# Expert weights through a ring of ten raw pieces, with the expert loops written out

## What is computed

```python
def ec_moe(h, router_w, w_gate, w_up, w_down):
    B, T, D = h.shape
    cap = EC_CAPACITY * T // N_EXPERTS
    aff = jax.nn.softmax(jnp.einsum('btd,de->bte', h, router_w, preferred_element_type=jnp.float32), axis=-1)
    gate, idx = lax.top_k(jnp.swapaxes(aff, 1, 2), cap)
    flat = idx.reshape(B, N_EXPERTS * cap)
    xg = jnp.take_along_axis(h, flat[..., None], axis=1).reshape(B, N_EXPERTS, cap, D)
    a = jax.nn.silu(jnp.einsum('becd,edf->becf', xg, w_gate)) * jnp.einsum('becd,edf->becf', xg, w_up)
    y = jnp.einsum('becf,efd->becd', a, w_down) * gate[..., None].astype(h.dtype)
    return jnp.zeros_like(h).at[jnp.arange(B)[:, None], flat].add(y.reshape(B, N_EXPERTS * cap, D))
```

## Time and profile before

| | |
|---|---|
| median of the runs | 1538.47 us |
| profiled execution, its own time | 1540.21 us |
| its span (first to last instruction) | 1538.4 us |
| PE busy | 1361.9 us, 89% |
| PE weight loads | 1012.9 us, 66% |
| DVE busy | 1017.8 us, 66% |
| ACT busy | 704.7 us, 46% |
| GpSimd busy | 295.8 us, 19% |
| DMA | 296.06 MB, mean 192 GB/s |
| expert stage | from the first gather at 932 to the end |

### The profile page before, as it was taken

The page is one execution under the profiler, slowest core; times in us unless marked ns, Lnnn a source line. Parts: engine busy times, 40 slices in busy tenths (PEclk is TensorE's granted clock), DMA queues, the critical chain, the costliest instruction groups (busy, mean ns, idle before and its releaser), DMA issues.

```text
span 1538.4 us, 18265 instructions
## 1 busy us (share of the span) xinstructions
PE 1361.9 (89%) x6828; PEld 1012.9 (66%) x6828; DVE 1017.8 (66%) x1093; ACT 704.7 (46%) x674; POOL 295.8 (19%) x193
## 2 busy tenths in 40 slices
PE   6888988799698989877889996999999999999995
PEld 1577868688696979662767763666666666666663
DVE  1766124543675959691425366999988999988993
ACT  2322234444334434431322103766667666776672
POOL 1021001111000000000000100135344444554422
PEclk9899989899799999958889967999999999999998
DMA  9403201112302121315106236999999999999992
GB/s 364 141 28 114 81 24 50 50 36 76 97 1 90 55 89 55 103 55 213 38 28 234 97 133 242 353 364 376 372 371 372 366 380 355 373 369 365 367 363 59
DMA packets 111843, 296.06 MB, mean 192 GB/s; under 512 B 7077, under 2 KB 33061, under 8 KB 111785
## 3 DMA queue, kind: packets, MB, share of 16 engines
q1 hardware_dynamic: 108264, 284.25, 50.7%
q0 software_dynamic: 3520, 11.01, 3.1%
HBM read 278.47 MB, written 16.78 MB: 192 GB/s over the span
## 4 chain that ended last, share of the span: by engine, by line
PE 69%; DVE 16%; issue 6%; ACT 6%; DMA 2%; POOL 1%; DVEq 0%; ACTq 0%; SPq 0%; POOLq 0%
PE ps L1547 18%; PE ps L1548 17%; PE ps L1549 17%; PE ps L1613 5%; PE ps L1717 4%; DVE w_lo L1474 3%; ACT w_hi L1016 2%; PE ps L1668 1%; DVE w_lo L1068 1%; ACT arena L841 1%; ACT w_hi L837 1%; DVE arena L1490 1%; DMA arena<-in_w_mod_dram 1%; PE ps L1792 1%; DVE arena L1117 1%
## 5 line engine op out<-in xcount | busy, mean ns | idle before, releaser
L1474 DVE TENSOR_TENSOR w_lo<-arena,w_hi 128x2048 fp32r<-128x2048 f32 x192 | 435.3, 2287 | 67.5 <-ACT w_hi L1016 49.9
L1547 PE MATMUL ps<-w_hi,act_hi 128*80 128x512 f32 (+1 forms) x1048 | 419.7, 401 | 32.1 <-DVE w_lo L1474 14.9
L1548 PE MATMUL ps<-w_lo,act_hi 128*80 128x512 f32 (+1 forms) x1048 | 414.9, 396 | 0.0
L1549 PE MATMUL ps<-w_hi,act_lo 128*80 128x512 f32 (+1 forms) x1048 | 413.6, 395 | 0.0
L1016 ACT ACTIVATE w_hi<-arena 128x2048 fp32r<-128x2048 f32 x180 | 343.4, 1915 | 141.7 <-PE ps L1549 141.7
L1547 PEld LDWEIGHTS ps<-w_hi,act_hi 128*80 128x80 f32 (+1 forms) x1048 | 169.0, 161 | 118.5 <-DVE w_lo L1474 29.7
L1549 PEld LDWEIGHTS ps<-w_hi,act_lo 128*80 128x80 f32 (+1 forms) x1048 | 168.7, 161 | 75.7 <-issue 1.6
L1548 PEld LDWEIGHTS ps<-w_lo,act_hi 128*80 128x80 f32 (+1 forms) x1048 | 169.0, 161 | 69.0 <-issue 1.2
L1547 PE MATMUL ps<-act_hi,w_hi 128*128 128x320 f32 x576 | 189.6, 329 | 5.3 <-DVE act_lo L1375 5.3
L1548 PE MATMUL ps<-act_lo,w_hi 128*128 128x320 f32 x576 | 183.5, 319 | 0.0
L1549 PE MATMUL ps<-act_hi,w_lo 128*128 128x320 f32 x576 | 183.2, 318 | 0.0
(11 more groups left out here) (195 smaller groups left out, 1385.8 us busy)
## 6 DMA issues: line engine op xcount, KB each, us to landing
arena<-in_w_exp_gate_dram SPq DMA_DIRECT2D x64, 1024.0 KB, 8.9
arena<-in_w_exp_up_dram SPq DMA_DIRECT2D x64, 1024.0 KB, 7.2
arena<-in_w_exp_down_dram SPq DMA_DIRECT2D x64, 1024.0 KB, 7.1
arena<-in_w_mod_dram SPq DMA_DIRECT2D x24, 1024.0 KB, 6.4
arena<-in_w_in_dram SPq DMA_DIRECT2D x18, 1024.0 KB, 5.5
arena<-in_w_in_dram SPq DMA_DIRECT2D x12, 512.0 KB, 4.7
gl_raw<-arena SPq DMA_DIRECT2D x32, 160.0 KB, 1.8
arena<-gl_raw SPq DMA_DIRECT2D x8, 640.0 KB, 8.0
```

Of the source, the lines that this page charges most:

```text
L1474: v.tensor_tensor(Wl[sl], eraw[slot], Wh[sl].bitcast(F32), ALU.subtract).then_inc(s_el, 1)
L1547: t.matmul(out, sh, mh, start=start, stop=False)
L1548: t.matmul(out, sh, ml, start=False, stop=False)
L1549: return t.matmul(out, sl, mh, start=False, stop=stop)
```

## The change

The raw ring gets ten pieces: one more over `v_hg` and G1 (slot 0), one over the end of the constants and the states (slot 7), and two in `X` behind the expert's temporaries (slots 8 and 9). Piece 0 is issued right behind the stores of x1, ahead of the stores of the normed rows. Pieces 1 to 3 go out where 0 to 2 did, 4 to 6 where 3 to 5 did; 7 waits for the second half of G2 to be made, 8 for the router's products, 9 for the top-k. From piece 10 on, SP waits for the low part of the piece ten before. All loops over experts are written out in Python, on all five engines. The converted ring keeps its three pairs (`EWh`, `EWl`, `NEW` are other names for the same).

```diff
@@ -203,8 +203,9 @@
         assert 4864 <= 5120
 
         G2s = G2
-        NRE = 6
-        eraw = [part(0, 2048), part(2048, 2048), part(4096, 2048)] + raw
+        eraw = [arena[:, o_vso:o_vso + 2048]] + [part(b, 2048) for b in (0, 2048, 4096)] + raw
+        eraw += [arena[:, o_st - 1024:o_st + 1024], part(7808, 2048), part(9856, 2048)]
+        NRE = len(eraw)
         ye = part(6144, 1024)
         xgt = part(7168, 640)
         xgt3 = xgt.rearrange("p (k t) -> p k t", k=KD)
@@ -217,6 +218,8 @@
         brow = arena[:, o_vso + 2048:o_vso + 2560]
         yq = [v_hg, arena[:, o_vso + 2560:o_vso + 5120].rearrange("p (i n) -> p i n", i=NT)]
         kctx = yq[1][:, 0, :]
+
+        EWh, EWl, NEW = Wh, Wl, NHL
 
         xh, xl = (w[:, 0, :].rearrange("p (k t) -> p k t", k=KD) for w in (act_hi, act_lo))
         xh1, xl1 = (w[:, 2, :].rearrange("p (k t) -> p k t", k=KD) for w in (act_hi, act_lo))
@@ -606,6 +609,14 @@
         def width(key):
             return 1024 if key[0] == "q" else 2048
 
+        def piece_of(n):
+            if n < 8:
+                return n // 4, 0, n % 4
+            e, j = (n - 8) // 12 + 1, (n - 8) % 12
+            if e == NE:
+                return 2, NE - 1, j
+            return j // 4, e - (j >= 8), j % 4
+
         block = ctx.enter_context(nc.Block())
 
         @block.sync
@@ -696,42 +707,38 @@
             for i in range(NT):
                 sp.wait_ge(s_x1, NT + i + 1)
                 sp.dma_start(y_tile[i], x1[:, i, :]).then_inc(s_yrow, 16)
+            wg, wu, wd = (A[n][0] for n in ("w_exp_gate", "w_exp_up", "w_exp_down"))
+
+            def epiece(n):
+                w, e, k = piece_of(n)
+                src = (wg, wu, wd)[w][e, 2 * P * k:2 * P * k + 2 * P, :].rearrange("(k p) n -> p k n", p=P)
+                sp.dma_start(eraw[n % NRE].rearrange("p (k n) -> p k n", k=2), src).then_inc(s_er[n % NRE], 16)
+
+            epiece(0)
             for i in range(NT):
                 sp.wait_ge(s_xn2, i + 1)
                 sp.dma_start(xn_rows[i * P:(i + 1) * P, :], xn2[i % 2]).then_inc(s_xrow[i % 2], 16)
             load(len(PIECES) - 1)
 
 
-            wg, wu, wd = (A[n][0] for n in ("w_exp_gate", "w_exp_up", "w_exp_down"))
-
-            def epiece(w, e, k, slot):
-                src = w[bass.ds(e, 1), bass.ts(k, 2 * P), :].rearrange("a (k p) n -> p (a k) n", p=P)
-                sp.dma_start(eraw[slot].rearrange("p (k n) -> p k n", k=2), src).then_inc(s_er[slot], 16)
-
-
             sp.wait_ge(s_yrow, 16 * NT)
             sp.wait_ge(s_xn2, NT)
             sp.wait_ge(s_sq2, NT)
-            for n in range(8):
-                if n == NRE - NRAW:
-                    sp.wait_ge(s_lo, len(SPLITS))
-                    sp.wait_ge(*used[("mod", LATE[-1], 1)])
-                if n >= NRE:
-                    sp.wait_ge(s_el, n - NRE + 1)
-                epiece(wg if n < 4 else wu, 0, n % 4, n % NRE)
-            with sp.Fori(1, NE) as e:
-                for j in range(12):
-
-                    sp.wait_ge(s_el, e * 12 + (j - 4 - NRE + 1))
-                    if j < 4:
-                        epiece(wg, e, j, (j + 2) % NRE)
-                    elif j < 8:
-                        epiece(wu, e, j - 4, (j + 2) % NRE)
-                    else:
-                        epiece(wd, e - 1, j - 8, (j + 2) % NRE)
-            for j in range(4):
-                sp.wait_ge(s_el, 188 + j - NRE + 1)
-                epiece(wd, NE - 1, j, (188 + j) % NRE)
+            for n in range(1, 4):
+                epiece(n)
+            sp.wait_ge(s_lo, len(SPLITS))
+            sp.wait_ge(*used[("mod", LATE[-1], 1)])
+            for n in range(4, 7):
+                epiece(n)
+            filled(sp, ("g2", LATE[-1]))
+            epiece(7)
+            filled(sp, ("rt",))
+            epiece(8)
+            sp.wait_ge(s_gi, 1)
+            epiece(9)
+            for n in range(NRE, 12 * NE):
+                sp.wait_ge(s_el, n - NRE + 1)
+                epiece(n)
             sp.wait_ge(s_scat, 32 * NE)
             sp.wait_ge(s_nk, 16)
             sp.wait_ge(s_nv, 16)
@@ -809,7 +816,7 @@
             gather(1)
             gather(2)
             pool.wait_ge(s_gt, 4)
-            with pool.Fori(2, NE - 1) as e:
+            for e in range(2, NE - 1):
                 gather(e + 1)
                 scatter(e - 2)
             for e in range(NE - 3, NE):
@@ -1011,15 +1018,16 @@
                         xhi(e + 1)
 
             def ehi_at(e, j):
-                act.wait_ge(s_er[(j + 2) % NRE], (e * 2 + (j - 4) // 6 + 1) * 16)
-                act.wait_ge(s_eu, e * 12 + (j - 6))
-                a.activation(Wh[(j + 2) % NHL], eraw[(j + 2) % NRE], ACT.Copy).then_inc(s_eh, 1)
+                n = e * 12 + j - 4
+                act.wait_ge(s_er[n % NRE], 16 * (n // NRE + 1))
+                act.wait_ge(s_eu, n - NEW + 1)
+                a.activation(EWh[n % NEW], eraw[n % NRE], ACT.Copy).then_inc(s_eh, 1)
 
             def ehi_first(n):
                 act.wait_ge(s_er[n % NRE], 16 * (n // NRE + 1))
-                if n >= NHL:
-                    act.wait_ge(s_eu, n - 2)
-                a.activation(Wh[n % NHL], eraw[n % NRE], ACT.Copy).then_inc(s_eh, 1)
+                if n >= NEW:
+                    act.wait_ge(s_eu, n - NEW + 1)
+                a.activation(EWh[n % NEW], eraw[n % NRE], ACT.Copy).then_inc(s_eh, 1)
 
             filled(act, ("out", 1, NT - 1))
             for n in range(NHL):
@@ -1032,13 +1040,13 @@
                     a.activation(aa[0:CAP, :], pair(0)[0:CAP, :], ACT.Silu).then_inc(s_silu, 1)
             xhi(1, xh1)
             body(1)
-            with act.Fori(2, NE - 1) as e:
+            for e in range(2, NE - 1):
                 body(e)
             body(NE - 1, last=True)
             for n in range(188, 192):
                 act.wait_ge(s_er[n % NRE], 16 * (n // NRE + 1))
-                act.wait_ge(s_eu, n - 2)
-                a.activation(Wh[n % NHL], eraw[n % NRE], ACT.Copy).then_inc(s_eh, 1)
+                act.wait_ge(s_eu, n - NEW + 1)
+                a.activation(EWh[n % NEW], eraw[n % NRE], ACT.Copy).then_inc(s_eh, 1)
                 if n == 188:
                     ahi(NE - 1)
 
@@ -1469,9 +1477,9 @@
                         link(v.tensor_copy(dst[:, :, CAP_LAT:CAP], src[:, :, 0:1].broadcast_to([P, KD, CAP_CTX])))
 
 
-            def elo(sl, ready, slot):
-                dve.wait_ge(s_eh, ready)
-                v.tensor_tensor(Wl[sl], eraw[slot], Wh[sl].bitcast(F32), ALU.subtract).then_inc(s_el, 1)
+            def elo(n):
+                dve.wait_ge(s_eh, n + 1)
+                v.tensor_tensor(EWl[n % NEW], eraw[n % NRE], EWh[n % NEW].bitcast(F32), ALU.subtract).then_inc(s_el, 1)
 
             def xmod(e):
                 dve.wait_ge(s_xgT, e + 1)
...
@@ -1517,25 +1525,25 @@
                         hidden(e, e * 12 + 4)
 
             for n in range(NHL):
-                elo(n % NHL, n + 1, n % NRE)
+                elo(n)
             xmod(0)
             xlo(0)
             for n in range(NHL, 8):
-                elo(n % NHL, n + 1, n % NRE)
+                elo(n)
                 if n == 6:
                     xmod(1)
             xlo(1, (xh1, xl1))
             body(1, first=True)
             body(2, second=True)
-            with dve.Fori(3, NE - 1) as e:
+            for e in range(3, NE - 1):
                 body(e)
             body(NE - 1, last=True)
-            elo(188 % NHL, 189, 188 % NRE)
+            elo(188)
             alo(NE - 1)
-            elo(189 % NHL, 190, 189 % NRE)
+            elo(189)
             yout(NE - 2)
-            elo(190 % NHL, 191, 190 % NRE)
-            elo(191 % NHL, 192, 191 % NRE)
+            elo(190)
+            elo(191)
             yout(NE - 1)
 
         @block.tensor
...
@@ -1860,18 +1868,18 @@
             turn_x(0)
             pe.wait_ge(s_xgl, 1)
             for n in range(8):
-                piece_mm(n // 4, n + 1, n % NHL, xh, xl, n % 4)
+                piece_mm(n // 4, n + 1, n % NEW, xh, xl, n % 4)
                 if n == 4:
                     pe.wait_ge(s_xgm, 1)
                     turn_x(1)
             body(1, first=True)
-            with pe.Fori(2, NE - 1) as e:
+            for e in range(2, NE - 1):
                 body(e)
             body(NE - 1, last=True)
             pe.wait_ge(s_alo, NE)
             pe.wait_ge(s_y, NE - 1)
             for q in range(4):
-                piece_mm(2, 189 + q, (188 + q) % NHL, ah, al, q)
+                piece_mm(2, 189 + q, (188 + q) % NEW, ah, al, q)
 
 
 # ---- launch: one core; inputs and outputs as the reference has them ----
```

More of the change, by code:

```diff
@@ L1504, in body @@
                 for j in range(12):
-                    elo((j + 2) % NHL, e * 12 + (j - 3), (j + 2) % NRE)
+                    elo(e * 12 + j - 4)
                     if j == 1 and first:
@@ L1819, in piece_mm @@
                 pe.wait_ge(s_el, ready)
-                wh, wl = (w[sl].rearrange("p (k n) -> p k n", k=2) for w in (Wh, Wl))
```

(3 more changed lines are left out.)

## The result

Over 16 runs of each kernel on one chip the changed kernel took 1543.37 us (1539.01 to 1548.06) and the kernel before 1538.61: a ratio of 1.0031 with an interval of 1.0019 to 1.0043. That is **4.8 us slower**, less than half a per cent and yet clear of no change. The forecast of 1538.1, 0.4 us faster than before, was 5.3 us too low and had the sign wrong; its range held the time.

What follows compares the result with a forecast made beforehand. It took PE, 97% busy and waiting for DVE's low parts, never for weights, to bound the expert stage. Loops -1.6 and piece 0 +1.2 made -0.4 us against the median of 1538.47: 1538.1, range 1531 to 1548.

Steps and rivals of the forecast that it cites:

- The ring: Expert stage, steady part: ten raw pieces for six change nothing, since no piece lands late; 0 us.
- Rival C: Expert stage: DMA sets the pace after all, so four more pieces of head start save 10.4 us, 1528; 8%.
- Loops written out: Expert loops: a DVE loop pass costs 0.13 us more than written-out code, over 12 passes; -1.6 us.
- Code fetch: Expert stage: about 16 more instruction-queue packets over 12 passes cost nothing; 0 us, upper bound +21.
- rival B: Expert stage: code supply for the written-out loops costs up to +21 us, about 1559; 6%.
- Rival D: Expert loops: each jump back stalls for a fetch that written-out code avoids, saving 15.6 us, 1523; 3%.
- Piece 0 ahead of the normed stores: Before the router: the first normed store lands late, DVE's third norm waits for its buffer; +1.2 us, bounds 0 and +2.5.
- Pieces 1 to 3 and the end: Pieces issued at 913, as three were before, and the stretch after the last expert's products: 0 us each.
- Six pieces ahead of the first gather: Ahead of the experts: three more pieces issued before the gather don't delay it; 0 us, ends -1.5 and +7.7.
- Rival A: Ahead of the experts: the first gather queues behind all six pieces, +7.7 us, 1545.8; 14%.
- The third norm at about 886: Sign to check: DVE's third norm, at 884.34 before the change, comes at about 886, 1.6 us late.
- the prediction's own sign: Test at the start of the experts: forecast wrong if the first product, expected at 946.3, moves by over 3 us.

Runs made afterwards that it cites:

- numbers 7 and 8: Fourth converted pair and moved token work: 7 on experiment 1's kernel with ring ten, 1516.75 us; 8 on the kernel before with ring six, 1515.63 us.
- experiment 3: The kernel before with only its loops over experts written out, ring of six and order of issues kept: 1539.49 us, 1.0003 of the kernel before.
- experiment 1: The changed kernel with piece 0 issued behind the stores of the normed rows, beside pieces 1 to 3: 1538.92 us, 1.0005 of the kernel before.
- Experiment 10: Experiment 1's kernel with two added 512 KB stores to a spare DRAM buffer where piece 0 had stood: 1541.78 us, measured in one run.
- Experiments 6 and 9: The changed kernel: 6 with a third buffer for the normed rows, 1538.82 us; 9 with piece 0 between the second and third normed store, 1538.59 us.
- experiment 2: The changed kernel with pieces 7 to 9 held until the first gather has landed: 1542.5 us, 1.0026 of the kernel before.
- experiment 5: Experiment 1's kernel with pieces 4 to 9 held until the first gather has landed: 1536.7 us, 0.9997 of the kernel before.
- experiments 5 and 11: 11: number 8 with pieces 3 to 5 held until the first gather landed and DVE's first token step before its third low part: 1509.18 us.
- experiment 4: Experiment 1's kernel with the first 512 KB of piece 0 back ahead of the normed stores, the rest behind: 1540.04 us, 1.0012 of the kernel before.

## Where the prediction was right, and the two terms that failed

Two terms of the sum failed, both on the low side: the price of piece 0 ahead of the stores (+1.2, measured +3.6 to +4.0) and the gain of the written-out loops (-1.6, measured 0). That the rest was 0 was right.

**The ring, 0: right.** ACT's waits are for PE alone, and numbers 7 and 8 show that ten raw pieces aren't worth more than six even at 34.16 us an expert. Rival C, that DMA sets the pace because its share is 1.0, is refuted by the same two.

**Loops written out, -1.6: wrong, 0.** This step failed by the row that I chose, and by how I read it: one distance of 35.70 in the earlier trace rows stood for what DVE's written-out code gives. The token step at 1032.23 is that of body(2), but the one at 1067.93 is that of body(3), the first pass of DVE's loop, so most of this distance ran in the loop. In experiment 3 the same pass takes 35.80, and so do its neighbours; twelve experts need 429.8 us, as before. In the changed kernel most distances are 35.77, and twelve take 429.48. Why two passes took 35.69 and 35.70 in the kernel before (996.54 to 1032.23 to 1067.93), and what the slow one of 36.0 waits for, was not settled. A difference of 0.13 us in one distance was no ground for a term of 12 times its size.

**Code fetch, 0: right.** 17 packets, no new wait: that is against rival B. Rival D, a stall at each jump back, falls with experiment 3, where the jumps are gone and nothing is gained.

**Piece 0 ahead of the normed stores, +1.2: the right mechanism, mis-sized.** The step named the place, the wait and who is behind it, and missed the sum: I reckoned that the store would land at 886, and it landed at 887.90. It measured +3.6 in the trace and 4.0 in the times of experiment 1. I had priced the piece by one with nothing of its queue in front (4.9 us) and the bytes at full rate. Experiment 10 shows that this was about right for bytes: behind as many bytes of stores the third norm is 1.2 us late, for the 1.6 that I had reckoned. The rest comes with the load among stores on their queue. From the 1.6 I had taken off 0.4, because PE was not free for the next router products any sooner. That was wrong too: PE began them 3.33 us later rather than 3.68, but they took 3.59 us for 3.24, and from the third norm to the router's end it is 20.44 us in both traces. So it is partly luck that experiment 10 gives the same 1.2 as my term. My upper bound of +2.5, a whole piece at full rate, was too low: it was taken from rows in which no load flew among stores. Experiments 6 and 9 settle that it is DVE's wait for this one buffer.

**Pieces 1 to 3 and the end, 0: right.**

**Six pieces ahead of the first gather, 0: right within what one gather can tell.** It took 0.72 us longer, but so much is scatter: with three pieces ahead the first gathers took 7.3, 7.8, 8.1 and 8.6 us (experiment 2, the kernel before, experiment 3, number 8), with six 7.7 to 8.5. Rival A, a gather queued behind all six, is refuted by this row: the piece issued 0.16 us before the gather landed 6.6 us after it.

```profile
arena<-in_w_exp_gate_dram SPq DMA_DIRECT2D x1, 1024.0 KB, 15.2
...
arena<-xn_rows,arena POOLq DMA_INDIRECT x1, 8.5
```

By the Trainium skill, "DMA: Bandwidth & Descriptors", section "Queues, rings and completion order", each DMA engine takes turns between the queue rows that have work for it. This row agrees: a piece asked for first was no barrier. Yet the gather is not free of the pieces. In nine of the ten traces that show it, it landed 0.1 to 0.2 us behind the third of the pieces issued ahead of it (1.3 in the changed kernel), which had gone out 2.9 to 3.5 us before it. So its 7 to 8 us go with those three, and not with the three behind them; why it lands with the third was not tried.

**The sum.** Put -1.6 at 0 and +1.2 at 4.0, add up to 0.7 for the gather, and the forecast becomes 1538.5 + 4.0 + 0.7 = 1543.2, for 1543.37. That it fits so well is luck, since the 4.0 has 2.4 us of uncertainty and the 0.7 is one gather's. Both wrong terms were too low, by 1.6 and by 2.4 to 2.8; with opposite signs in the forecast they added up to about nothing and made it look like no change. "The third norm at about 886" was the line that told: it stood at 888.0. By the prediction's own sign it was wrong, too: the first product came at 949.46 for 945.06, 4.4 us later, where over 3 was to count against it.

## What to carry to other kernels

Before a prefetch is put ahead of a store, ask who waits for that store to give back its buffer, and let the last such store go first; a third buffer does as well, and either is worth about 4 us here. A deeper ring is worth nothing while its consumer never waits for a landing: count the waits for landings, not the busy share of DMA, and deepen the ring whose return the consumer waits for (here the converted one; with the token work moved, 21 to 22 us). When a stall ahead of a stage is shortened, look at what the next engine does in that time, or the gain stops there, as 2.4 of 3.6 us did in experiment 5.

## What the hardware showed that I had not expected

**A load among stores of one queue slows both.** 1 MB of load took 7.3 us where a piece with no store about took 4.9, and a 512 KB store behind it 7.9, for 4.9 behind as many bytes of stores; 306 GB/s for 405. The share of busy DMA time doesn't show it, at 0.96. The stores alone were run once; other queues and sizes were not tried.

**An idle set of DMA engines nearly halves a gather:** 4.2 and 4.3 us with nothing else in flight (experiments 5 and 11), 7.3 to 8.6 with three to six pieces.

**A DMA share of 1.0 is no bound.** From 977 to 1480 it stood at 1.01 in the kernel before, at 368 GB/s, and at 1.01 with the fourth pair, at 381 and 384.

**PE's clock scatters the total.** The modulation rows ahead of the gather ran in 8.20 and 8.74 us in the kernel before, where the granted clock was 0.85 and 0.81 on the mean, and in 9.33 and 9.54 in the profiled run of experiment 4, where it was 0.74 and 0.73. That made them outlast the top-k, and the gather went out 2.5 us later after the third norm, which a late norm can seem to cost. What sets the clock from run to run was not tried.
